# A hybrid trunk layer with a 16-expert stage on one Trainium2 core: y kept by token tiles, expert 0's weights loaded into its memory during the output projection, router logits from raw rows, expert 0's rows named ahead of the others', one low piece on Pool, and the last rows reordered

## What is computed

```python
x = x + mod_lat[:, 2] * mix_x                      # mix_x = concat(y_a, y_p, y_f) @ w_out
h = modulate(rms_norm(x, norm_ffn_g), mod_lat[:, 3], mod_lat[:, 4])
lg = h @ rg_w + rg_b                               # 4 groups, the best one is taken
le = h @ re_w + re_b                               # 16 experts, the 2 best of the group
gates = sum(one_hot(ids) * w_e)                    # two gates per token
for e in range(16):                                # (1024 x 512), (1024 x 512), (512 x 1024)
    y = y + gates[:, e:e+1] * ((silu(h @ wg[e]) * (h @ wu[e])) @ wd[e])
x = rms_norm(x + mod_lat[:, 5] * y, final_norm_g)
```

## Time and profile before

| | |
|---|---|
| median of 3 runs | 1000.93 us (998.99 to 1002.23) |
| the profiled execution, its time | 997.77 us |
| its span | 995.3 us |
| TensorE busy | 859.6 us (86%) |
| VectorE busy | 641.7 us (64%) |
| ScalarE busy | 419.2 us (42%) |
| Pool busy | 201.2 us (20%) |
| HBM read, written | 172.26 MB, 24.64 MB |

### The profile page before, as it was taken

How to read it: one execution, slowest core, us unless ns; L and a number is a source line. 1 busy time by engine, 2 the same in 40 slices (tenths; PEclk the granted TensorE clock), 3 DMA queues, 4 the chain that set the end, 5 groups by cost and what they waited for, 6 DMA issues and landing times.

```text
span 995.3 us, 11255 instructions
## 1 busy us (share of the span) xinstructions
PE 859.6 (86%) x3521; PEld 604.4 (61%) x3522; DVE 641.7 (64%) x684; ACT 419.2 (42%) x499; POOL 201.2 (20%) x187
## 2 busy tenths in 40 slices
PE   5679999975979898999736799999999999999960
PEld 2254454432534455888635688788887888788850
DVE  2133578998689135433368579677887579946746
ACT  2242542533444423111235257446656358524543
POOL 1000380980000000000001223222142113432210
PEclk9899999996989999999857899999999999999995
DMA  8922601403520460332266769986997799966774
GB/s 291 352 45 106 232 21 67 144 0 104 167 85 4 169 253 22 127 112 100 85 253 217 289 216 375 318 254 183 360 378 212 236 295 392 365 192 190 259 246 189
DMA packets 91909, 196.70 MB, mean 198 GB/s; under 512 B 10739, under 2 KB 31345, under 8 KB 91884
## 3 DMA queue, kind: packets, MB, share of 16 engines
q1 hardware_dynamic: 83500, 165.98, 46.4%
q0 software_dynamic: 7056, 25.15, 10.0%
q10 hardware_dynamic: 1328, 5.24, 1.3%
HBM read 172.26 MB, written 24.64 MB: 198 GB/s over the span
## 4 chain that ended last, share of the span: by engine, by line
PE 57%; DVE 19%; DMA 11%; issue 6%; ACT 4%; DVEq 1%; POOL 1%; POOLq 0%; SPq 0%; ACTq 0%
PE bank L711 10%; PE bank L890 5%; PE bank L892 5%; PE bank L891 5%; DMA mixed_rows<-ysc,idg 3%; DMA mring<-in_mod_w 3%; PE bank L824 3%; PE bank L826 3%; PE bank L825 3%; DMA xg<-normed_rows,idg 3%; PE bank L911 3%; PE bank L913 3%; PE bank L912 3%; DVE WP L1545 2%; PE bank L693 2%
## 5 line engine op out<-in xcount | busy, mean ns | idle before, releaser
L711 PE MATMUL bank<-hT,wring 128*128 128x512 f32 x384 | 166.8, 593 | 2.6 <-ACT hT L971 1.9
L1545 DVE TENSOR_TENSOR WP<-raw,WP 128x2048 fp32r<-128x2048 f32 x64 | 145.5, 2290 | 30.6 <-ACT WP L1139 29.9
L890 PE MATMUL bank<-WP,xp 128*128 128x512 f32 x368 | 146.9, 399 | 3.3 <-issue 1.9
L1139 ACT ACTIVATE WP<-raw 128x2048 fp32r<-128x2048 f32 x64 | 122.8, 1919 | 56.2 <-PE bank L892 51.5
L892 PE MATMUL bank<-WP,xp 128*128 128x512 f32 x368 | 145.1, 394 | 0.0
L891 PE MATMUL bank<-WP,xp 128*128 128x512 f32 x368 | 145.0, 394 | 0.0
L711 PEld LDWEIGHTS bank<-hT,wring 128*128 128x128 f32 x384 | 72.7, 190 | 91.9 <-issue 88.5
L628 POOL COPY idg<-gid 128x1 int32 (+1 forms) x24 | 11.4, 476 | 500.8 <-DVE gid L1534 301.7
L1550 DVE TENSOR_TENSOR WP<-raw,WP 128x1024 fp32r<-128x1024 f32 x64 | 76.0, 1224 | 10.0 <-ACT WP L1143 7.6
L890 PEld LDWEIGHTS bank<-WP,xp 128*128 128x128 f32 x368 | 70.2, 191 | 18.2 <-issue 2.3
L892 PEld LDWEIGHTS bank<-WP,xp 128*128 128x128 f32 x368 | 69.9, 190 | 14.8
(11 more groups left out here) (264 smaller groups left out, 1360.3 us busy)
## 6 DMA issues: line engine op xcount, KB each, us to landing
...
```

Source lines behind the costliest of these rows:

```text
L711: mm = pe.matmul(o_, wring[:, n % 3, k, :], src, start=k == 0, stop=k == KD - 1)
L890: pe.matmul(bank[g][:], x_hi, w_hi, start=k == 0, stop=False)
L1139: A_(WP[:, j, 0, 0:2 * D], raw[:, j, 0:2 * D], ACT.Copy).then_inc(s_hgu, 1)
L1545: tt(WP[:, j, 1, 0:2 * D], raw[:, j, 0:2 * D], WP[:, j, 0, 0:2 * D].bitcast(F32), ALU.subtract).then_inc(s_logu[j], 1)
```

## The change

- `yT`, `y_hi` and `y_lo` are laid out by token tiles, so that a tile's memory is free when the tile is projected. Expert 0's four gate and up pieces go there, loaded by SP after tiles 1 and 3; the first is split within the projection.
- TensorE transposes `x1` itself, half a row at a time, not the normed row. The scale of the modulation is multiplied into the router's weights (`rw2`), the root is applied to the logits, and the shift's part is computed once (`shb`) in the Fourier stage. `logits` runs one tile behind; the last tile's halves are interleaved with the last projection.
- Expert 0's token numbers come directly from its ranks: a one-hot `oh0`, 16 small bf16 matmuls, `gid0`, and Pool gathers with it, without its pick. Its rows are split ahead of the rest of the lists.
- The full lists are made with bf16 one-hots in two steps: token numbers as two exact parts, 32 matmuls, after the second piece of expert 0; gates as three bf16 parts, 48 matmuls, after the fourth. Before, it was one sum in f32.
- The low half of expert 0's piece 1 is made by Pool once all logits are there; piece 2's and 3's stand later in VectorE's list, expert 0's down pieces later still. The small tables move to Pool.
- At the end, VectorE norms tiles 0 to 3 before it waits for the last gathers, and ScalarE waits for the read-back rows in pairs. Some linking operations are gone.
- The slots' loop is as before, with new tile names and one count less in Pool's chain.

The diff, cut to its core:

```diff
-        yT = at("yT", [P, KD, SEQ], F32, o)
+        yT = at("yT", [P, NT, KD, P], F32, o)
...
-        y_hi = at("y_hi", [P, KD, SEQ], F32R, rec0 + 35840)
+        y_hi = at("y_hi", [P, NT, KD, P], F32R, rec0 + 32768)
         w_lo = at("w_lo", [P, KD, D], F32R, PHASE)
-        y_lo = at("y_lo", [P, KD, SEQ], F32R, PHASE + 32768)
+        y_lo = at("y_lo", [P, NT, KD, P], F32R, PHASE + 32768)
...
+        Y0, H0 = PHASE + 32768, rec0 + 32768
+        raw_gu = [at(f"raw_gu{j}", [P, 2 * D], F32, (Y0, H0)[j % 2] + 8192 * (j // 2)) for j in range(KE)]
+        GU = [(Y0 + 16384, H0 + 16384), (Y0 + 24576, H0 + 24576), (PHASE, PHASE + 8192), (PHASE + 16384, PHASE + 24576)]
+        gu = [[at(f"gu{j}_{n}", [P, 2 * D], F32R, GU[j][n]) for n in range(2)] for j in range(KE)]
+        dn = [[at(f"dn{j}_{n}", [P, D], F32R, PHASE + 73728 + 8192 * j + 4096 * n) for n in range(2)] for j in range(KE)]
+        raw_dn = [at(f"raw_dn{j}", [P, D], F32, rec0 + 4096 * j) for j in range(KE)]
+        xp = at("xp", [P, 2, 2, KD, P], F32R, rec0 + 16384)
+        rv = at("rv", [P, 2, 2 * NT, NS], BF16, rec0 + 24576)
+        rg = at("rg", [P, 3, 2 * NT, NS], BF16, rec0 + 28672)
+        ysc = at("ysc", [P, 2, D], F32, PHASE + 65536)
+        oh = at("oh", [P, 2 * NT, P], BF16, PHASE + 65536)
+        oh0 = at("oh0", [P, NT, P], BF16, PHASE + 65536 + 4096)
...
-                sp.wait_ge(s_x1, t + 1)
+                sp.wait_ge(s_x1, 2 * t + 2)
                 sp.dma_start(x1v[:, t], xr[t % NX][:]).then_inc(s_x1d[t % NX], 16)
                 sp.wait_ge(s_xn, t + 1)
                 sp.dma_start(xnv[:, t], xs[t % 2][:]).then_inc(s_xnd[t % 2], 16)
                 if t + NX < NT:
                     sp.wait_ge(s_x1d[t % NX], 16 * (t // NX + 1))
+                    sp.wait_ge(s_t2, 2 * t + 2)
                     sp.dma_start(xr[t % NX][:], xv[:, t + NX]).then_inc(s_xr[t % NX], 16)
-
-
-            def load_gate_up(e, j):
-                for g, w in enumerate((wg, wu)):
-                    sp.dma_start(raw[:, j, g * D:(g + 1) * D].rearrange("p (k n) -> p k n", n=HALF),
-                                 w[0, EORD[e]][2 * P * j:2 * P * (j + 1), :].rearrange("(k p) n -> p k n", p=P))\
-                        .then_inc(s_rgu[j], 16)
-
-            def load_down(e, j):
-                sp.dma_start(raw[:, j, 2 * D:], wd[0, EORD[e]][j * P:(j + 1) * P, :]).then_inc(s_rdn[j], 16)
+                if t in (1, 3):
+                    load_gate_up(0, t - 1)
+                    load_gate_up(0, t)
...
+            pool.wait_ge(s_lg, NT)
+            pool.wait_ge(s_hgu, 2)
+            pool.tensor_tensor(gu[1][1][:], raw_gu[1][:], gu[1][0][:].bitcast(F32), ALU.subtract).then_inc(s_logu[1], 1)
             for n in range(2):
                 pool.wait_ge(s_xnd[n], 16 * (NT // 2))
             pool.wait_ge(s_gid, 1)
-            gather(0, 0)
+            pool.indirect_dma_start(out=xg[:], out_offset=None, in_=xn_d,
+                                    in_offset=bass.IndirectOffsetOnAxis(ap=gid0[:], axis=0)).then_inc(s_xg, 16)
+
+
+            pool.wait_ge(s_cnt, 1)
+            row = lambda a, n: rs[0:1, a:a + n]
+            inc1, eT, lT = row(1200 + 2 * NE, NE), row(1400, TAB), row(1440, TAB)
+            link(pool.memset(lT, 0.0))
+            link(pool.tensor_tensor(lT[:, 0:TAB - 1], eT[:, 1:TAB], eT[:, 0:TAB - 1], ALU.subtract))
+            link(pool.tensor_copy(tab[0:1, 0, :], eT))
+            link(pool.tensor_copy(tab[0:1, 2, :], lT))
+            pool.tensor_copy(tab[0:1, 3, 0:1], inc1[:, NE - 1:NE]).then_inc(s_tab, 1)
+            pool.wait_ge(s_gid, 2)
...
+                if k == 2:
+                    pe.wait_ge(s_py, 4)
+                    pe.wait_ge(s_scr, 1)
+                    for j in range(2 * KD):
+                        src = (scr, shr)[j // KD]
+                        mm = pe.transpose(bank[6][:, 2 * j:2 * j + 2], src[0:2, j % KD * P:(j % KD + 1) * P],
+                                          ident[0:2, 0:2])
+                    mm.then_inc(s_ct, 1)
+                if k == 5:
+                    pe.wait_ge(s_shb, 1)
+                    for j in range(KD):
+                        mm = pe.matmul(bank[7][:, 0:NG + NE], shb[:, j, :], rw[:, j, :], start=j == 0,
+                                       stop=j == KD - 1)
+                    mm.then_inc(s_cp, 1)
...
+            for t in range(NT):
+                out_half(t, 0)
+                if t >= 1:
+                    turn(t - 1, 0)
+                    turn(t - 1, 1)
+                if t < NT - 1:
+                    out_half(t, 1)
+                    if t >= 1:
+                        logits(t - 1, 0)
+                        logits(t - 1, 1)
+
+
+            out_half(NT - 1, 1, range(0, 3))
+            logits(NT - 2, 0)
+            logits(NT - 2, 1)
+            turn(NT - 1, 0)
+            out_half(NT - 1, 1, range(3, KD))
+            logits(NT - 1, 0)
+            turn(NT - 1, 1)
+            logits(NT - 1, 1)
...
+            pe.wait_ge(s_oh0, 1)
+            for t in range(NT):
+                pe.matmul(bank[0][:, 0:1], oh0[:, t, :], tokb[:, t:t + 1], start=t == 0, stop=False)
+                mm = pe.matmul(bank[0][:, 0:1], oh0[:, t, :], tokb[:, 2 * NT:], start=False, stop=t == NT - 1)
+            mm.then_inc(s_id0, 1)
...
+            gate_up(0, 0, 0)
+            gate_up(0, 0, 1)
+            slot_ids()
+            for j in range(2, KE):
                 gate_up(0, 0, j)
+            slot_gates()
...
+            square_half(NT - 1, 0)
+            take_turned(NT - 1, 0)
+            square_half(NT - 1, 1)
+            take_turned(NT - 1, 1)
+            root(NT - 1)
+            for j in range(1, KE):
+                hi_gate_up(0, j)
...
+            dve.wait_ge(s_ct, 1)
+            link(dve.tensor_copy(colt[:], bank[6][:, 0:4 * KD].rearrange("p (j g) -> p j g", g=2)[:, :, 0]))
+            dve.wait_ge(s_rw, 64)
+            tt(rw2[:], rw[:], colt[:, 0:KD].unsqueeze(2).to_broadcast([P, KD, NG + NE]), ALU.mult)
+            dve.tensor_copy(shb[:], colt[:, KD:].unsqueeze(2).to_broadcast([P, KD, P])).then_inc(s_shb, 1)
+            dve.wait_ge(s_cp, 1)
+            tt(rb[:], bank[7][:, 0:NG + NE], rb[:], ALU.add)
...
+            for t in range(NT):
+                xb, tmp = xr[t % NX], xm[t % 2]
+                dve.wait_ge(s_xr[t % NX], 16 * (t // NX + 1))
+                if t >= 2:
+                    dve.wait_ge(s_ss2, 2 * t - 2)
+                for h in range(2):
+                    hs = slice(h * HALF, (h + 1) * HALF)
+                    dve.wait_ge(s_mix, 2 * t + h + 1)
+                    tt(tmp[:, hs], bank[(2 * t + h) % 4][:], g2[:, hs], ALU.mult).then_inc(s_mixu, 1)
+                    dve.wait_ge(s_mixu, 2 * t + h + 1)
+                    tt(xb[:, hs], xb[:, hs], tmp[:, hs], ALU.add).then_inc(s_x1, 1)
+                if t == NT - 1:
+                    take_logits(t - 1)
+                dve.wait_ge(s_ss2, 2 * t + 2)
+                ts(stat[:, 44 + t:45 + t], stat[:, 10 + 2 * t:11 + 2 * t], stat[:, 11 + 2 * t:12 + 2 * t], 1.0 / D,
+                   ALU.add, ALU.mult).then_inc(s_ms2, 1)
+                dve.wait_ge(s_rt2, t + 1)
+                link(dve.reciprocal(stat[:, 44 + t:45 + t], stat[:, 44 + t:45 + t]))
+                if 1 <= t < NT - 1:
+                    take_logits(t - 1)
+                if t >= 2:
+                    dve.wait_ge(s_xnd[t % 2], 16 * (t // 2))
+                link(stt(out=xs[t % 2][:], in0=xb[:], scalar=stat[:, 44 + t:45 + t], in1=scr[:], op0=ALU.mult,
+                         op1=ALU.mult))
+                tt(xs[t % 2][:], xs[t % 2][:], shr[:], ALU.add).then_inc(s_xn, 1)
+                if t == 6:
+                    lo_gate_up(0, 0)
+            take_logits(NT - 1)
...
+            key0 = every(1380, NT)
+            mk3 = mk[:].rearrange("p (t e) -> p t e", e=NE)
+            link(stt(out=key0, in0=mk3[:, :, 0], scalar=-8192.0,
+                     in1=bank[4][:, 0:P].rearrange("p (t e) -> p t e", e=NE)[:, :, 0], op0=ALU.mult, op1=ALU.add))
+            stt(out=oh0[:], in0=K("iota").unsqueeze(1).to_broadcast([P, NT, P]), scalar=-8192.0,
+                in1=key0.unsqueeze(2).to_broadcast([P, NT, P]), op0=ALU.add, op1=ALU.is_equal).then_inc(s_oh0, 1)
...
+            dve.wait_ge(s_id0, 1)
+            ts(gid0[:], bank[0][:, 0:1], -1.0, 0.0, ALU.add, ALU.max).then_inc(s_gid, 1)
...
+            for r in range(2):
+                lo_rows(0, 0, r)
+            for n in range(2):
+                dve.wait_ge(s_xnd[n], 16 * (NT // 2))
+            tt(rv[:, 0], so[:], K("tok128").unsqueeze(2).to_broadcast([P, 2 * NT, NS]), ALU.mult)
+            ts(rv[:, 1], so[:], K("tokp"), None, ALU.mult).then_inc(s_oh, 1)
+            lo_gate_up(0, 2)
+            big = rs[0:1, 1560:1560 + TAB * NE].rearrange("p (s e) -> p s e", e=NE)
+            eT = rs[0:1, 1400:1400 + TAB]
+            link(tt(big, sq_[0:1].unsqueeze(1).to_broadcast([1, TAB, NE]),
```

(48 more changed lines are left out.)

346 lines of the change are left out of this document (175 added, 171 removed).

## The result

The changed kernel takes **985.42 us** (median of 4 runs, 984.47 to 988.47) against 999.96 for the kernel before in the same runs (998.21 to 1002.23): ratio 0.986, 95% interval 0.983 to 0.989. The profiled execution has a span of 984.2 us and a time of 986.19 of its own. So from profile to profile the span fell by 11.1 us and the time by 11.6, where 12.0 were forecast. From median to median it fell by 14.5 in these runs, and against the 1000.93 from which the forecast of 988.9 started by 15.5.

What follows compares the result with a forecast made beforehand. It took one serial chain of 72 us between projection and slot 1 as the bound, plus the tail. Handover -6.8 and tail -5.2 gave -12.0 from 1000.93, so 988.9 us; own range 986 to 992, widened to 983 to 997.

Steps and rivals of the forecast that it cites:

- Before L: Everything up to the last logits (L): work added and moved ahead, logits 0.7 us earlier, at 498.0 us.
- L to M: From last logits (L) to router masks (M): Pool's subtraction holds up VectorE's second router operation, +4.4 us.
- Rival 1: Between last logits and masks, VectorE's linked operations keep Pool out; the 4.4 us is not paid: 984.5 us, chance 0.16.
- M to G: From masks (M) to expert 0's first matmul (G): lists and one gather latency leave the path, 27.2 becomes 13.6 us.
- G to slot 1: From expert 0's first matmul (G) to slot 1's: deferred list and gate work lengthens it, 22.8 becomes 25.9 us, +3.1.
- Rival 2: Between expert 0's first matmul and slot 1, lists, gates or gather are late: 2 to 6 us more, 993, chance 0.17.
- rival 4: At slot 1, waiting for expert 1's weights leaves no change in effect: 1000 us, chance 0.06.
- rival 5: In expert 0, bursts with gaps keep TensorE at the low clock, costing 20 us: 1009 us, chance 0.06.
- The loop: The slots' expert loop: it should shift as a block and stay as long as before.
- Tail: At the end, final row pairs 0 and 1 come before the wait for the last gathers: 5.2 us saved.
- rival 3: The tail does not gain because loads of 4 MB and the gathers set it: 994 us, chance 0.08.
- The conversion to a time: The 12.0 us summed on the profiled execution were subtracted unchanged from the median of 1000.93, giving 988.9 us.

Runs made afterwards that it cites:

- experiment 1: The changed kernel with expert 0's low piece 1 made by VectorE behind the masks instead of by Pool: 986.49 us, ratio 0.988.
- Experiments 5 and 6: Low piece 1 on VectorE as in experiment 1, plus at the last logits a Pool fill of an unused buffer (986.48 us) or a Pool copy into it (989.14 us).
- Experiment 2: The changed kernel with Pool's first gather waiting for the full lists, which are built ahead of expert 0 again: 996.31 us, ratio 0.998.
- Experiment 4: The changed kernel with expert 0's weights loaded behind the last stored rows as before the change, and no pieces on Pool: 990.25 us, ratio 0.992.
- second profile: Profile of the changed kernel run once more, unaltered: 986.44 us, ratio 0.987.
- experiment 3: The changed kernel with VectorE's old order at the end, the sum that waits for the last gathers before the final row pairs: 994.6 us, ratio 0.995.

## Why the prediction was right, point by point

- **Before L: -0.7 forecast, -0.92 measured.** The last projection matmul ends at 490.80 (490.9 was worked out), and the last logits at 497.80, 7.0 us behind it (7.1). L differs by up to 5 us between the profiles of the changed kernel and its relatives, more than this term; that it was met so closely is partly luck.
- **L to M: +4.4 forecast, +4.24 measured.** One operation of 4.38 us, M at 507.69 (508). Rival 1, Pool kept out, did not come: Pool's subtraction was under way 0.18 us before VectorE's operation, and experiment 1 shows the price by taking the cause away. Experiments 5 and 6 tell which kind of Pool work pays it.
- **M to G: -13.6 forecast, -13.96 measured** (27.46 to 13.50, from the start of the masks). The steps: ids at M + 4.4 (4.5); Pool starts the gather 0.94 us after they are written (0.2 was too little); rows at M + 10.0. VectorE is free for them at M + 12.1, just as worked out. The chain of waits goes through it and not through the gather (start us, us, what):

```profile
516.87 2.29 DVE oh L1667
519.16 0.66 DVE so L1669
519.84 0.50 DVE xp L1633
```

so the 0.7 us that the gather was late cost nothing. Experiment 2: with its early ids unused, L to G is 10.1 us longer, of which up to 2.6 are the price of the unused list. Experiment 4: without the early weights about half of the handover's gain remains.
- **G to slot 1: +3.1 forecast, +3.00 measured.** Of its parts, the 32 list matmuls took 0.83 (1.3), the gates' 1.38 (1.9), the register loads 2.2 (1.5): the errors cancel. Rival 2, a late second start, did not come, nor did rival 4 (in front of slot 1 TensorE waits 1.93 us for nothing that the profile names, not for weights), nor rival 5: the 24 matmuls of the first two pieces took 7.95 us (529.14 - 521.19), as long as before (8.1), and the loop's clock is 0.99.
- **The loop: 0 forecast, +0.74 measured.** TensorE waits four times for a gather (2.10, 2.03, 2.24 and 0.72 us) instead of three (2.15, 2.20, 2.22). The prediction had let it shift as a block; it shifts by 6.9 of 7.6 us.
- **Tail: -5.2 forecast, -4.19 measured,** and -5.56 in the second profile. The mechanism was right (rival 3 falls with experiment 3), and the size is uncertain by as much as two profiles differ. In the first profile row pair 0 starts 4.7 us after D, as worked out; the 1.0 us that is missing lies behind pair 1, where VectorE waits 0.74 us for the gathers and 0.55 for ScalarE, and the sum had neither. The five experiments that leave the tail alone (1, 2, 4, 5, 6) have 19.74 to 20.80 us from D to R, around the 20.3 that was forecast (25.5 - 5.2).
- **The conversion to a time** was the largest error. The sum was right to 0.4 us between the times of the two profiled executions (11.6 against 12.0) and to 0.9 between their spans (11.1). Part of this is luck: loop and tail gave 1.75 us less than forecast, the other terms together 0.84 more. But the one of before lay 3.2 us under the median that I started from, and I carried that distance over; the one of the changed kernel lies 0.8 us above its median. 11.6 + 3.2 + 0.8 are the 15.5, within rounding. Both distances are of the size of the spread before L.
